# Twelve of the sixteen block differences of each down phase on GpSimd in place of VectorE

## The reference

```python
def squared_relu_mlp(u, w_up, w_down):
    return jnp.square(jax.nn.relu(u @ w_up)) @ w_down

# in layer i, behind the mixer
f = squared_relu_mlp(rmsnorm(h, norm_mlp_pre[i]), w_up[i], w_down[i])
h = h + rmsnorm(f, norm_mlp_post[i])
```

## Time and profile before

| | us |
|---|---|
| median of 3 runs | 1300.36 (1300.06 to 1302.87) |
| the profiled execution | 1299.86 |
| its span | 1298.1 |
| PE busy | 1282.3 |
| DVE busy | 812.4 |
| ACT busy | 655.7 |
| POOL busy | 161.8 |

### The profile page before, as it was taken

The page is one execution under the profiler, slowest core; times in us unless marked ns, Lnnn a source line. Parts: engine busy times, 40 slices in busy tenths (PEclk is TensorE's granted clock), DMA queues, the critical chain, the costliest instruction groups (busy, mean ns, idle before and its releaser), DMA issues.

```text
span 1298.1 us, 17991 instructions
## 1 busy us (share of the span) xinstructions
PE 1282.3 (99%) x6743; PEld 1058.0 (81%) x6743; DVE 812.4 (63%) x1160; ACT 655.7 (51%) x1141; POOL 161.8 (12%) x195
## 2 busy tenths in 40 slices
PE   9999999999999999999999999999999999999998
PEld 7777778888778988888888888777788888888886
DVE  5676686888544633346787964776473334478887
ACT  6645355676543423235555743775453323355663
POOL 0046353462000000000000000000000000000000
PEclk9999999999999999999999999999999999999999
DMA  7588875343763468758966527656224778669854
GB/s 249 158 266 259 221 176 153 106 166 131 216 154 101 146 198 203 215 171 219 256 197 194 177 68 174 129 114 151 76 81 113 228 174 214 223 188 247 250 170 155
DMA packets 110367, 230.01 MB, mean 177 GB/s; under 512 B 8134, under 2 KB 18646, under 8 KB 110038
## 3 DMA queue, kind: packets, MB, share of 16 engines
q1 hardware_dynamic: 84240, 159.93, 37.7%
q0 software_dynamic: 21760, 67.11, 24.0%
q10 hardware_dynamic: 4294, 2.00, 0.9%
HBM read 225.69 MB, written 70.04 MB: 228 GB/s over the span
## 4 chain that ended last, share of the span: by engine, by line
PE 89%; DVE 4%; DMA 3%; ACT 2%; issue 1%; DVEq 0%; SPq 0%; ACTq 0%
PE G L1983 47%; PE G L2414 4%; PE G L2412 4%; PE G L2410 4%; PE X L2006 3%; PE X L2414 3%; PE X L2410 3%; PE X L2412 3%; PE X L2064 3%; PE X L1983 3%; DMA raw<-in_ssd_w_in 2%; PE G L2064 2%; PE X L2170 1%; PE X L2179 1%; PE X L2253 1%
## 5 line engine op out<-in xcount | busy, mean ns | idle before, releaser
L1289 DVE TENSOR_TENSOR wlo<-raw,whi 128x1024 fp32r<-128x1024 f32 x143 | 176.7, 1235 | 288.9 <-ACT whi L704 288.6
L1983 PE MATMUL G<-uhi,whi 128*128 128x512 f32 x736 | 294.4, 400 | 2.2 <-DVE sz L1414 2.0
L1983 PE MATMUL G<-uhi,wlo 128*128 128x512 f32 x736 | 287.0, 390 | 0.0
L1983 PE MATMUL G<-ulo,whi 128*128 128x512 f32 x736 | 286.7, 390 | 0.0
L704 ACT ACTIVATE whi<-raw 128x1024 fp32r<-128x1024 f32 x143 | 151.5, 1060 | 248.7 <-PE G L1983 161.2
L1112 ACT ACTIVATE whi<-raw 128x1024 fp32r<-128x1024 f32 x112 | 118.2, 1058 | 122.9 <-PE G L2414 51.0
L1757 DVE TENSOR_TENSOR wlo<-raw,whi 128x1024 fp32r<-128x1024 f32 x112 | 135.3, 1220 | 66.3 <-ACT whi L1112 66.1
L1983 PEld LDWEIGHTS G<-uhi,whi 128*128 128x128 f32 x736 | 138.2, 188 | 33.4 <-issue 2.6
L1983 PEld LDWEIGHTS G<-uhi,wlo 128*128 128x128 f32 x736 | 138.2, 188 | 29.6 <-DVE wlo L1337 0.2
L1983 PEld LDWEIGHTS G<-ulo,whi 128*128 128x128 f32 x736 | 138.3, 188 | 28.3
L609 POOL DMA_DIRECT2D tsum<-in_w_down x32 | 32.9, 1039 | 653.5 <-PE G L1983 539.9
(11 more groups left out here) (371 smaller groups left out, 2471.3 us busy)
## 6 DMA issues: line engine op xcount, KB each, us to landing
tsum<-in_w_down POOLq DMA_DIRECT2D x48, 1024.0 KB, 10.2
raw<-in_w_up SPq DMA_DIRECT2D x64, 512.0 KB, 3.9
raw<-tsum SPq DMA_DIRECT2D x64, 512.0 KB, 3.9
raw<-in_w_down SPq DMA_DIRECT2D x48, 512.0 KB, 4.6
raw<-in_ssd_w_in SPq DMA_DIRECT2D x20, 512.0 KB, 4.4
raw<-in_w_mem_kv SPq DMA_DIRECT2D x16, 512.0 KB, 3.7
raw<-in_ssd_w_out SPq DMA_DIRECT2D x16, 512.0 KB, 4.4
raw<-in_swa_w_in SPq DMA_DIRECT2D x16, 512.0 KB, 4.2
```

The source lines that it names most:

```text
L1289: dve.tensor_tensor(wlo[q][:, :, :], raw[q % 2][:, :, :], whi[q][:, :, :].bitcast(F32), ALU.subtract).then_inc(lo_done, 1)
L1983: mm = pe.matmul(o, st, mv, start=(kt == 0 and fresh and not go_on), stop=(q == total - 1 and k == 1), skip_group_check=True)
```

## The change

Three things change. The twelve differences with x = 2, 4 and 3 are issued by POOL in place of DVE, behind all 24 weight sums of the layer. They stand in one loop, x = 2 first, then x = 4, then x = 3. Only x = 2 waits for a left operand (M3's, by chunk); x = 4 and x = 3 wait for x = 2's chunk alone, and the places that `SUMS_AT` gave them are gone. The four differences with x = 1 stay on DVE at their places. And since POOL takes its instructions in order and the differences stand behind the weight sums, layer 1's last four weight sums are issued behind panels 218, 220, 222 and 224 in place of 222, 228, 234 and 240.

```diff
-SUMS_AT = {(M5, 1): (1, 3), (M2, 3): (2, 0), (M2, 5): (2, 1), (M2, 7): (2, 2), (M3, 1): (2, 3),
-           (M3, 5): (4, 0), (M3, 7): (4, 1), (M1, 3): (4, 2), (M1, 5): (4, 3),
-           (M4, 3): (3, 0), (M4, 7): (3, 1), (M7, 3): (3, 2), (M7, 5): (3, 3)}
-W1_SUM_AT = tuple(range(162, 176, 2)) + tuple(range(190, 216, 2)) + (222, 228, 234, 240)
+W1_SUM_AT = tuple(range(162, 176, 2)) + tuple(range(190, 216, 2)) + (218, 220, 222, 224)
...
                     ps.wait_ge(panel_done, p)
                     weight_sum(i, n)
+                for x, out_at, minus in ((2, (0, 1), (1, 1)), (4, (0, 0), (0, 1)), (3, (1, 0), (0, 1))):
+                    for c in range(4):
+                        if x == 2:
+                            ps.wait_ge(left_lo_done, 28 * i + 4 * M3 + c + 1)
+                        ps.wait_ge(left_sum, 16 * i + 4 + c + (1 if x > 2 else 0))
+                        ps.tensor_tensor(chunk_of(out_at, c), chunk_of(out_at, c), chunk_of(minus, c),
+                                         ALU.subtract).then_inc(left_sum, 1)
...
-                    if x > 1:
-                        dve.wait_ge(left_sum, 16 * i + 4 * SUM_RANK[x] + c - 3)
...
-                        if (r, q) in SUMS_AT:
-                            left_sums(*SUMS_AT[r, q])
+                        if (r, q) == (M5, 1):
+                            first_left_sum(3)
```

More of the change, by code:

```diff
@@ L1742, in mlp, with first_left_sum @@
                     relus(0, j)
[L1744 to L1748, removed]
-                    if x > 1:
-                        dve.wait_ge(left_sum, 16 * i + 4 * SUM_RANK[x] + c - 3)
-                    dve.tensor_tensor(chunk_of(out_at, c), chunk_of(out_at, c), chunk_of(minus, c),
+                def first_left_sum(c):
+                    dve.wait_ge(hidsq_done, 36 * i + 4 * (4 + c) + 8)
+                    dve.tensor_tensor(chunk_of((1, 1), c), chunk_of((1, 1), c), chunk_of((1, 0), c),
                                       ALU.subtract).then_inc(left_sum, 1)
@@ L1769, in mlp @@
                     if j > 0:
-                        left_sums(1, j - 1)
+                        first_left_sum(j - 1)
                     relus(1, j)
@@ L1777, in mlp @@
                 right_lo(2)
-                left_sums(1, 2)
+                first_left_sum(2)
                 relus(1, 3)
```

## The result

The changed kernel takes 1330.06 us (median of 4, 1329.62 to 1330.84) against 1300.26 for the kernel before (4 runs). The ratio is 1.0221, 95% interval 1.0206 to 1.0237: slower by 29.8 us. I had forecast 1308 and a range of 1300 to 1318. The sign was right and the size was not.

The account below looks back on a forecast made before the run. PE bounds the kernel, so DVE's relief is hidden. Waits of 3.2 us in layer 0 and 5.0 in layer 1, less 0.5 at the boundary, add 7.7 to 1299.86: forecast 1308, 8-in-10 range 1300 to 1318.

Parts of the forecast that it names:

- What bounds the kernel: Whole kernel: PE, busy 99% of the span; taking work off DVE in the phases gains nothing, being hidden.
- Turns between DVE and POOL: Down phases: a POOL difference and a DVE operation with two SBUF inputs shut each other out and run alternately.
- The hold: Down phases: each POOL difference of 1024 elements takes 1.77 us of DVE's time and gives 1.14 back.
- my first rival: POOL's plain subtraction is slower than line 592, with a hold of 2.1 us: 1312.7 us; chance 0.14.
- the cycle: Down phases: one POOL difference plus one DVE operation in turns, 1.77 + 1.14 = 2.9 us.
- the stretch: Each down phase: eight x = 4 and x = 3 differences back to back on POOL, 23.2 us; layer 0 from about 651.
- the lead: How far DVE runs ahead of PE: 5.6 us at best, 4.8 in layer 0's stretch, 2.8 in layer 1's.
- My upper bound for an unknown hold: A hold of 2.98 us: PE waits 10.1 us in layer 0 and 12.1 in layer 1, giving 1322.
- The weight sums: Layer 1: four earlier sums cost nothing beyond the 5.0 us; a rival, late loads alone, gave 1304.9, chance 0.06.
- Layer 1: Down phase of layer 1: PE waits 5.0 us, chosen between 3.2 and 5.6.
- The boundary: Behind layer 0: the two differences leaving DVE in M7 let it run earlier, 0.5 us gained.

Follow-up runs that it names:

- the memset kernel: Layer 0's twelve differences on POOL replaced by a memset of the same size, layer 1 as before the change: 1299.81 us, against 1300.08 for the kernel before.
- the layer-0-alone kernel: Against the kernel before, only layer 0's twelve differences go to POOL; layer 1 keeps its on DVE and its weight sums' old places: 1311.91 us, ratio 1.0090.
- the sums-alone kernel: Against the kernel before, only layer 1's last four weight sums move, to panels 218, 220, 222, 224; all differences stay on DVE: 1306.04 us, ratio 1.0046.
- the spaced kernel: All twelve differences per layer on POOL, x = 4 and x = 3 held for panels 21 to 45, never two in a row: 1310.79 us against 1299.82 before.
- the far-apart kernel: Differences on POOL, x = 4 and x = 3 held for panels 20 to 38 in layer 0, 29 to 39 in layer 1: 1308.94 us against 1300.08 before.
- the kernel with the sums at their old places: The changed kernel with layer 1's last two weight sums back at panels 234 and 240, between the differences: 1318.46 us against 1299.82 before the change.

## Why the prediction was wrong, point by point

**What bounds the kernel: right.** The loss is all in PE's waits in the two phases and in what follows them. Taking 12 differences off DVE gained nothing, as the memset kernel shows.

**Turns between DVE and POOL: right.** Each of POOL's differences stands against one DVE operation of two SBUF inputs, `w_sum` is untouched, and without reads on POOL there is no loss. The Trainium skill's lock (SBUF — State Buffer, section "SBUF: two separate sides") agrees. It counts only against a GpSimd operation that reads SBUF, as the memset shows. By the same section of the Trainium skill the holder keeps the ports "for the whole instruction"; for one input the runs differ from that, 0.83 of 2.79 us, and the measurement decides.

**The hold: mis-sized, 1.77 us predicted and 2.2 measured.** "I take 1.77 because two rows of the same kind of operation set it": they were not of the same kind, since an input that repeats its values is cheaper to read. This was my first rival. What I held against it, that lines 592 and 664 have "one slope", is no evidence: two rows always give one slope. With 2.2 us the cycle is 3.3 in place of 2.9, nine in a row in place of eight, and the stretch 29.0 in place of 23.2 us. By my own sum DVE then loses 9 x 2.2 = 19.8 us, gets back some 4 x 1.14 = 4.6 and 3.9 x 29.0 / 23.2 = 4.9 of idle time, and the lead covers 4.8: 5.5 us of waiting. PE idled for 6.7, and for 7.9 in the layer-0-alone kernel. So the right hold explains most of the idle time and the method comes some 1 to 2 us short. My upper bound for an unknown hold, 10.1 us in this layer, covers the idle time, but not the 10.5 by which the phase grew.

**What a stop costs behind itself: missing from the sum, and its largest error.** I counted PE's idle time alone and put what follows a stop at nothing, without a reason. Layer 0 is 10.5 us longer for 6.7 of idle time, layer 1 is 19.3 longer for 13.0: 3.8 and 6.3 us come on top. Two things make them up. A stop costs something even at the full clock. In the sums-alone kernel five waits, 4.2 us together, made the phase 5.7 us longer with the clock at 1.00, so 0.3 a stop. (0.17 of it is that the page shows a matmul for 0.39 where the next could start at 0.227.) By this estimate the three stops of layer 0 cost 0.9 and the ten of layer 1 3.0. That leaves 2.9 and 3.3 us for matmuls at the lower clock, which PE ran twice in each phase. The layer-0-alone kernel fits: four waits of 7.9 us and one stretch at the lower clock in place of two, and its phase is 10.5 longer as well. Over the kernel PE's busy time grew by 10.9, more than a third of the loss, 10.1 of it in the phases. That the clock falls because PE stood still is read from the order of the rows: it never falls in a phase without a stop. The length of the stop alone doesn't decide it. The two long stops of each phase after (3.3, 2.85, 3.6 and 2.6 us) were followed by 0.50 or close to it, and in the spaced kernel so was one of 2.0:

```profile
728.50:730.50 2.00, 2.00 (x6) 1.54 (x6) 2.00 (x3) 0.00 (x0) 0.00 (x0) 0.50 0.96 346
```

In the far-apart kernel stops of 2.1 and 2.3 us were not, nor was the spaced kernel's other stop of 2.0, nor the one of 2.7 us in the layer-0-alone kernel:

```profile
676.00:678.00 2.00, 1.68 (x9) 1.06 (x7) 2.00 (x2) 0.00 (x0) 2.00 (x2) 1.00 0.73 246
```

So this term can be bounded in a forecast, some 1 to 2 us a long stop or nothing, and 0.3 for any stop, and not pinned down.

**The weight sums: the step that failed in its mechanism.** "That the sums come earlier is itself costed at nothing beyond this": by themselves they cost 5.7 us of phase, 4.2 of it waits. I gave each of four sums 11.6 us to land and saw them as done before the differences began. What I didn't ask is what four at once do to the loads between them. A `raw` load takes 13.5 us beside them where it took 5.9, and `whi` comes every 4.1 us for a panel of 2.72. Six such panels are over 8 us behind, against a lead of 5.6 at best. The argument that the stage's DMA share is 0.69 was an average over 158 us, and in 1160 to 1200 us of the sums-alone kernel it is 0.89.

**Layer 1: 5.0 predicted, 19.3 measured.** The sums-alone kernel puts 5.7 of it on the sums. The other 13.6 is the nine differences on a DVE that comes out of the late loads without a lead, with the clock on top. Layer 0 pays 10.5 for the same nine. That the two parts add up is worked out and was not run: the kernel with the sums at their old places also broke the nine in two, and lost 7.5. The time after against that of layer 0 alone, 1330.06 - 1311.91 = 18.2, agrees with the phase within 1.2 us. The lead was also thinner than I had read it: I took 2.8 us at panel 28, but in the kernel before it was 1.8 at panel 20 and 1.2 at panel 24, inside the stretch.

**The boundary: 0.5 gained was predicted, nothing seen.** PE's wait there was 2.18 us. After:

```profile
PE G L2064 <- DVE wlo L1293: 2.2, 1, 2.2
```

**In the sum.** Predicted 3.2 + 5.0 - 0.5 = 7.7. Measured +10.5 and +19.3, together 29.8, so 22.1 are missing. 10.1 of them came behind the stops, 6.2 by the lower clock and 3.9 by the stops themselves, as estimated above. Of the other 12.0, the hold and the ninth difference explain 2.3 (5.5 - 3.2) in layer 0 and, if it is alike there, 2.3 in layer 1. The waits of the sums are 4.2 and the gain at the boundary that did not come is 0.5. The last 2.7 us are not assigned by these runs.

## What to carry to other kernels

Work moved to GpSimd isn't off VectorE if both read two SBUF tensors: at 1024 elements each difference took 2.2 us of DVE's time to save 1.1. What decides is whether they stand one after another or a few panels apart, against the lead: the same twelve cost layer 0 10.5 us in a row and nothing far apart. Price an operation from a row with the same kind of operands, ask for each moved transfer what else is loading then, and when a sum ends in TensorE waiting, allow 0.3 us more for each stop, and for stops of 2 us and more, slow matmuls behind them.

## What the runs showed of the hardware that I had not expected

- GpSimd's two-input subtraction of 128x1024 takes 2.39 us alone, a multiplication by a constant 2.79, a memset 0.96. They hold off a VectorE operation with two SBUF inputs for 2.2, at most 0.83, and 0 us.
- A repeated input is cheaper: 1469 against 1850 ns at 768 elements.
- After a wait of 3.3 us TensorE ran its matmuls at the lower clock for about 3 us (restart at 663.17, granted clock 0.50 up to 666.0, 1.00 from 666.5); stops of 2.0 to 2.9 us came with and without such a fall, and in the sums-alone kernel five waits of at most 1.2 us left the granted clock of the stretch at 1.00, yet cost 0.3 us each beside the wait.
- One 1 MB addition in DRAM lands in about 12 us; four issued 5.4 to 5.7 us apart take 14.9 each and stretch the 512 KB loads beside them from 5.9 to 13.5 us.
